# Recurrent merges ahead of the spatial gate, later context transposes and expert shares, and four pieces of elementwise work on GpSimd

## What is computed

```python
y_a = fox_attention(...);  y_b = rg_lru(xb, ...);  y_c = nsa_attention(...);  y_d = spatial_gating(ud, vd, ...)
ys = stack([y_a * silu(ga), y_b * silu(gb), y_c * silu(gc), y_d * silu(gd)], axis=2)
proj = einsum('bsnw,nwd->bsnd', ys, w_branch)                    # n: the four branches
merged = sum(sigmoid(mg.reshape(B, S, 4, D)) * proj, axis=2)     # mg = norm(x) @ w_in[:, mg]
x = x + merged @ w_out
```

```python
x = x + grid_sincos(L)
hc = modulate(rmsnorm(ctx, ...), ...);  keys and values of the context -> state s_f, s_b     # gated linear attention
x = x + mod * mixer_output(...)
gp = probs[idx] / sum(probs[idx])                                # idx: the two chosen experts, gp: their shares
x = x + mod * sum_e gp_e * expert_e(h)
```

## Time and profile before

| | |
|---|---|
| median of 3 runs | 1083.97 us (1081.85 to 1086.04) |
| the profiled execution | 1090.9 us, of which the core's span is 1088.8 us |
| mean granted TensorE clock | 0.955 |
| busy: PE, PEld, DVE, ACT, POOL | 1007.3, 764.9, 612.8, 441.5, 49.5 us |
| chain that ended last | PE 75%, DVE 14%, DMA 6%, ACT 3%, issue 2% |
| HBM read | 221 MB |

### The profile page before, as it was taken

How to read it: one execution, slowest core, us unless ns; L and a number is a source line. 1 busy time by engine, 2 the same in 40 slices (tenths; PEclk the granted TensorE clock), 3 DMA queues, 4 the chain that set the end, 5 groups by cost and what they waited for, 6 DMA issues and landing times.

```text
span 1088.8 us, 13871 instructions
## 1 busy us (share of the span) xinstructions
PE 1007.3 (93%) x5638; PEld 764.9 (70%) x5638; DVE 612.8 (56%) x1065; ACT 441.5 (41%) x709; POOL 49.5 (5%) x66
## 2 busy tenths in 40 slices
PE   7999989999997998898979999995989999999984
PEld 5688667775896988678967886895965753566521
DVE  4777736563655455326574898666842511597605
ACT  4356532954664443124464101335632300556401
POOL 2000000000000000000010222000000000000010
PEclk8999989999998999899989999997899999999987
DMA  9634676765424744624322134002978997999993
GB/s 302 201 135 148 218 267 232 255 224 206 167 78 155 260 166 155 232 86 156 109 95 92 53 141 155 1 1 68 398 292 303 350 382 284 399 404 404 407 350 142
DMA packets 110413, 230.66 MB, mean 212 GB/s; under 512 B 8300, under 2 KB 15757, under 8 KB 110350
## 3 DMA queue, kind: packets, MB, share of 16 engines
q1 hardware_dynamic: 104144, 216.44, 54.8%
q0 software_dynamic: 2880, 9.71, 2.3%
q10 hardware_dynamic: 3326, 3.63, 1.1%
HBM read 221.11 MB, written 8.65 MB: 211 GB/s over the span
## 4 chain that ended last, share of the span: by engine, by line
PE 75%; DVE 14%; DMA 6%; ACT 3%; issue 2%; ACTq 0%; DVEq 0%
PE bank L791 9%; PE bank L1532 7%; PE bank L1533 7%; PE bank L1534 7%; PE bank L2595 6%; PE bank L756 5%; PE bank L2534 4%; PE bank L2535 4%; PE bank L2536 4%; PE bank L2619 3%; DMA more_slots<-in_moe_w_up 2%; PE bank L1446 2%; PE bank L2527 2%; PE bank L1575 2%; PE bank L967 1%
## 5 line engine op out<-in xcount | busy, mean ns | idle before, releaser
L1532 PE MATMUL bank<-rounded 128*128 128x256 f32 (+1 forms) x656 | 201.8, 308 | 9.0 <-DVE slot_rounded L680 4.3
L1533 PE MATMUL bank<-rounded 128*128 128x256 f32 x592 | 168.4, 284 | 0.0
L1532 PEld LDWEIGHTS bank<-rounded 128*128 128x128 f32 x656 | 126.3, 192 | 21.2 <-issue 9.7
L1534 PE MATMUL bank<-rounded,slot_rounded 128*128 128x256 f32 x472 | 134.8, 286 | 0.0
L791 PE MATMUL bank<-x_and_h,slot 128*128 128x256 f32 x544 | 129.1, 394 | 4.9 <-ACT x_and_h L595 4.9
L791 PEld LDWEIGHTS bank<-x_and_h,slot 128*128 128x128 f32 x544 | 106.1, 198 | 22.4 <-issue 7.7
L1533 PEld LDWEIGHTS bank<-rounded 128*128 128x128 f32 x592 | 113.9, 192 | 1.2 <-issue 1.0
L1522 DVE TENSOR_TENSOR slot_rounded<-slot,rounded 128x1024 fp32r<-128x1024 f32 (+1 forms) x63 | 67.1, 1086 | 68.9 <-ACT rounded L1516 68.7
L1534 PEld LDWEIGHTS bank<-rounded,slot_rounded 128*128 128x128 f32 x472 | 91.3, 193 | 0.0
L839 ACT ACTIVATE arena<-bank 128x256 f32<-128x256 f32 x56 | 21.4, 384 | 118.0 <-PE bank L791 96.3
L1516 ACT ACTIVATE rounded<-slot 128x1024 fp32r<-128x1024 f32 (+1 forms) x63 | 57.7, 943 | 27.0 <-PE bank L1534 23.3
(11 more groups left out here) (493 smaller groups left out, 2067.4 us busy)
## 6 DMA issues: line engine op xcount, KB each, us to landing
slot<-in_w_in SPq DMA_DIRECT2D x26, 2048.0 KB, 8.0
slot<-in_ada_w SPq DMA_DIRECT2D x12, 2048.0 KB, 8.4
slot<-in_moe_w_down SPq DMA_DIRECT2D x11, 2048.0 KB, 16.1
more_slots<-in_moe_w_gate SPq DMA_DIRECT2D x8, 2048.0 KB, 15.4
more_slots<-in_moe_w_up SPq DMA_DIRECT2D x8, 2048.0 KB, 18.2
slot<-in_moe_w_gate SPq DMA_DIRECT2D x7, 2048.0 KB, 9.9
x_and_h<-in_moe_w_up SPq DMA_DIRECT2D x6, 2048.0 KB, 15.2
more_slots<-in_moe_w_down SPq DMA_DIRECT2D x5, 2048.0 KB, 17.6
```

The source lines that it names most:

```text
L1532: t.do.matmul(dst, w_hi, x_hi, start=start, stop=False)
L1533: t.do.matmul(dst, w_hi, x_lo, start=False, stop=False)
L1534: return t.do.matmul(dst, w_lo, x_hi, start=False, stop=stop)
```

## The change

Five edits:
1. In `fill` the eight merges of branch 1 move ahead of the gd projections and the four `spatial` products. `merge_start` 1 now stands right behind `spatial_norm` and `h1_split`; `merge_start` 3 stands behind the last `spatial`. As the list over which `ada` is spread is eight jobs shorter, the `ada` jobs lie closer together, and the whole weave from about 107 us on shifts.
2. Of the context, each pair of `ctx_turn` stands one or two projections later.
3. The addition of positions goes from VectorE to GpSimd.
4. For branches 3, 0 and 2, GpSimd makes the low part of the gate's weights (21 instructions of 128x1024); the branch's own low part stays with VectorE. The waits change with it.
5. The shares are computed behind the first two one-hot matrices; scratch buffers are chosen so that the one-hot vectors survive.

```diff
-        spatial = [*ud[2:], *tokens("vd"), ("spatial_norm",), *channels("gd"), *[("spatial", j) for j in range(WT)]]
+        spatial = [*ud[2:], *tokens("vd"), ("spatial_norm",)]
+        gated = [*channels("gd"), *[("spatial", j) for j in range(WT)]]
...
-        fill, scored = spread(early + lru + spatial, ada, 10) + merge[1], attention(UNITS)
+        fill, scored = spread(early + lru + spatial, ada, 10) + merge[1] + gated, attention(UNITS)
...
-        PLAN += woven([*channels("cf0"), ("ctx_scan", 0), ("ctx_turn", 0, 0), ("ctx_turn", 0, 1),
-                       *channels("cf1"), ("ctx_scan", 1), ("ctx_turn", 1, 0), ("ctx_turn", 1, 1), *tokens("cv"),
+        PLAN += woven([*channels("cf0"), ("ctx_scan", 0), ("channels", "cf1", 0), ("ctx_turn", 0, 0), ("channels", "cf1", 1),
+                       ("ctx_turn", 0, 1), *channels("cf1")[2:], ("ctx_scan", 1), ("tokens", "cv", 0), ("ctx_turn", 1, 0), ("tokens", "cv", 1), ("ctx_turn", 1, 1),
                        ("ctx_state", 0), ("ctx_state", 1)], merge[0])
...
-            before = {3: ("merge", 1, KT - 1), 0: ("merge", 3, KT - 1), 2: ("merge", 0, KT - 1)}.get(n, ("merge", n, 0))
+            before = {3: PLAN[PLAN.index(("spatial", WT - 1)) + 1], 0: ("merge", 3, KT - 1), 2: ("merge", 0, KT - 1)}.get(n, ("merge", n, 0))
...
-        @part(VECTOR, "placed")
-        def vector_placed(v):
-            v.wait_ge(*at("position_in"))
-            v.wait_ge(*now("h1"))
-            v.do.tensor_tensor(xT[:, :, :], xT[:, :, :], merged, ALU.add).then_inc(*inc("x_placed"))
+        @part(GPSIMD, "placed")
+        def gpsimd_placed(g):
+            g.wait_ge(*at("position_in"))
+            g.wait_ge(*at("h1", KT - 1))
+            g.do.tensor_tensor(xT[:, :, :], xT[:, :, :], merged, ALU.add).then_inc(*inc("x_placed"))
...
+        def low_name(job, name):
+
+            return "split_gate_low" if job[0] == "merge" and job[1] != BRANCHES[0] and topic_of(name) == "mg" else "split_weights_low"
+
+        def gpsimd_split(g, job):
+            q = SPLITS.index(job)
+            for high, piece, low, name in pieces(job):
+                if low_name(job, name) == "split_gate_low":
+                    g.wait_ge(*at("split_weights_high", q, topic_of(name)))
+                    g.do.tensor_tensor(low, piece, high.bitcast(F32), ALU.subtract).then_inc(*inc("split_gate_low", q, topic_of(name)))
+
+        @part(GPSIMD, "merge_start")
+        def gpsimd_merge_start(g, n):
+            gpsimd_split(g, ("merge", n, 0))
+
+        @part(GPSIMD, "merge")
+        def gpsimd_merge(g, n, dt):
+            job = ("merge", n, dt)
+            if next_split(job):
+                gpsimd_split(g, next_split(job))
+
         def vector_split(v, job):
             q = SPLITS.index(job)
             for high, piece, low, name in pieces(job):
+                if low_name(job, name) == "split_gate_low":
+                    continue
...
-                t.wait_ge(*at("split_weights_low", q, "mg"))
+                t.wait_ge(*at(low_name(job, ("mg", n)), q, "mg"))
...
             v.do.tensor_tensor(chosen, oh1, oh2, ALU.add).then_inc(*inc("moe_chosen"))
-
-
-            for which, oh in enumerate((oh1, oh2)):
-                v.do.tensor_tensor(tmp16, oh, prob, ALU.mult).then_inc(*inc("router_steps"))
...
-            v.do.tensor_tensor(share, share, bcast(total, 1, 2), ALU.mult).then_inc(*inc("router", "shares"))
-
...
-                v.do.tensor_tensor(oh, oh, slot_of, ALU.mult).then_inc(*inc("router_steps"))
+                v.do.tensor_tensor((tmp16, pick)[which], oh, slot_of, ALU.mult).then_inc(*inc("router_steps"))
                 v.wait_ge(*now("router_steps"))
-                v.do.tensor_reduce(slot[:, which], oh, AX_X, ALU.add).then_inc(*inc("router_steps"))
+                v.do.tensor_reduce(slot[:, which], (tmp16, pick)[which], AX_X, ALU.add).then_inc(*inc("router_steps"))
...
             onehot(0)
             onehot(1)
+
+
+            for which, oh in enumerate((oh1, oh2)):
+                v.do.tensor_tensor((tmp16, pick)[which], oh, prob, ALU.mult).then_inc(*inc("router_steps"))
...
+            v.do.tensor_tensor(share, share, bcast(total, 1, 2), ALU.mult).then_inc(*inc("router", "shares"))
+
             gathered(0)
```

More of the change, by code:

```diff
@@ L2810, in vector_experts @@
             v.do.tensor_tensor(chosen, oh1, oh2, ALU.add).then_inc(*inc("moe_chosen"))
-            for which, oh in enumerate((oh1, oh2)):
-                v.do.tensor_tensor(tmp16, oh, prob, ALU.mult).then_inc(*inc("router_steps"))
-                v.wait_ge(*now("router_steps"))
-                v.do.tensor_reduce(share[:, which], tmp16, AX_X, ALU.add).then_inc(*inc("router_steps"))
-                v.wait_ge(*now("router_steps"))
-            v.do.tensor_tensor(total, share[:, 0], share[:, 1], ALU.add).then_inc(*inc("router_steps"))
-            v.wait_ge(*now("router_steps"))
-            v.do.reciprocal(total, total).then_inc(*inc("router_steps"))
-            v.wait_ge(*now("router_steps"))
-            v.do.tensor_tensor(share, share, bcast(total, 1, 2), ALU.mult).then_inc(*inc("router", "shares"))
             for tt in range(NT):
@@ L2893, in vector_experts @@
             onehot(1)
+            for which, oh in enumerate((oh1, oh2)):
+                v.do.tensor_tensor((tmp16, pick)[which], oh, prob, ALU.mult).then_inc(*inc("router_steps"))
+                v.wait_ge(*now("router_steps"))
+                v.do.tensor_reduce(share[:, which], (tmp16, pick)[which], AX_X, ALU.add).then_inc(*inc("router_steps"))
+                v.wait_ge(*now("router_steps"))
+            v.do.tensor_tensor(total, share[:, 0], share[:, 1], ALU.add).then_inc(*inc("router_steps"))
+            v.wait_ge(*now("router_steps"))
+            v.do.reciprocal(total, total).then_inc(*inc("router_steps"))
+            v.wait_ge(*now("router_steps"))
+            v.do.tensor_tensor(share, share, bcast(total, 1, 2), ALU.mult).then_inc(*inc("router", "shares"))
             gathered(0)
```

## The result

| | before | after |
|---|---|---|
| median of four runs each | 1083.18 us (1081.85 to 1086.04) | 1095.67 us (1094.18 to 1099.51) |
| profiled execution, its span | 1090.9, 1088.8 us | 1097.1, 1095.3 us |
| granted TensorE clock | 0.955 | 0.954 |

The ratio is 1.0096 (95% interval 1.0063 to 1.0129): the changed kernel is 10.4 us slower (7 to 14), where 3.8 us faster was forecast. A second comparison further down gives 1.0090. So I read from the traces where time goes, stretch by stretch, and take from the medians how much an edit costs.

What follows compares the result with a forecast made beforehand. TensorE, busy for 93% of the span, was taken as the bound. The terms 7.9 - 11.6 - 2.5 + 3.9 + 10.0 - 2.5 - 2.6 + 1.2 gave +3.8 us off 1084.0, forecast 1080; range 1068 to 1092.

Steps and rivals of the forecast that it cites:

- three signs that the prediction set for itself: Wrong if the stop inside merge 1 0 is missing, the position add leaves VectorE alone, or a GpSimd split exceeds 3 us.
- Edit 1, the stops: Load stop ahead of merge 3 0 goes (+7.9 us); new stops of 9.4 in merge 1 0, 1.8 in merge 3 0.
- Edit 1, the early half: Compression, ada jobs shifted: stops of 2.83, 1.37 and 0.84 us go, 2.2 for xb comes; +3.9 us, -1 to +7.
- Edit 1, what is late next: Behind the products, merge 3 0 stops 1.8 us, -2.5 with slow clock; no later merge of branch 3 got a stop.
- Edit 2: Context: both scan stops, 2.35 and 3.81 us, go with slow clock behind; +10.0 us, bounds 7 to 11.
- Edit 3: Position add: GpSimd takes 4.2 us and holds VectorE 4.1, 1.4 + 0.2 come back; net -2.5 us, +1.4 to -4.4.
- Edit 4: Gate low parts: three stops in branch 2's merges, -1.5 us, and the context's norm 1.1 later; sum -2.6 us.
- Rival C: GpSimd bounds the merges, rounded low parts priced at 3.7 us a piece; 1090 us, chance 12%.
- Edit 5: Shares leave the chain from expert choice to one-hot matrices, 1.36 us; counts late next by 0.15; +1.2 us.
- A: VectorE is not held through GpSimd's position add; 1076 us, chance 15%.
- B: The new stop at merge 1 0 is half as long, ScalarE and VectorE being less loaded; 1074 us, chance 20%.
- D: Loads bind the compression: xb and ada 3 to 6 each 2 us late, slow clock behind; 1088 us, chance 10%.

Runs made afterwards that it cites:

- second comparison: The unchanged changed kernel timed once more against the kernel before: +9.8 us (7.1 to 12.4).
- that half alone: Kernel before with only the ada jobs spread as in the changed kernel; gd, products and merges of branch 1 stay: +2.2 us (-0.9 to 5.3) against before.
- eight pieces: Changed kernel with GpSimd's position addition cut into eight of 256 elements instead of one of 2048: +8.0 us (5.2 to 11.0) against the kernel before.
- the kernel with filler passes: Kernel before with edit 1, the gate passes of merge 1 0 issued three times to fill its stop: +11.3 us (4.9 to 17.7) against before.
- the kernel with ud as cover: Kernel before with edits 1, 2 and 5, ud's last two projections moved behind the norm after vd: -8.5 us (-11.8 to -5.2) against before.

## Why the prediction was wrong, point by point

None of the three signs that the prediction set for itself came: the stop inside merge 1 0 is there, VectorE was held, and a split took 2.4 us. It failed by terms beside those that it watched.

**Edit 1, the stops: right.** 9.62 for 9.4, 2.32 for 1.8, and no load stop at merge 3 0. ScalarE's and VectorE's rows of the changed kernel show the chain that was written down (the exponentials at 284.71, the high part of ys 1, the low parts):

```profile
284.71 0.40 ACT L993 ACTIVATE arena<-arena 128x128 f32<-128x128 f32 x1 [4.82 <-DVE arena L985]
...
285.50 1.04 ACT L1582 ACTIVATE rounded<-arena 128x1024 fp32r<-128x1024 f32 x1
```

```profile
286.57 1.23 DVE L1588 TENSOR_TENSOR rounded<-arena,rounded 128x1024 fp32r<-128x1024 f32 x1 [1.89 <-ACT rounded L1582]
287.71 2.42 DVE L1546 TENSOR_TENSOR slot_rounded<-slot,rounded 128x512 fp32r<-128x512 f32 x3
```

**Edit 1, the early half: failed.** "+3.9; from -1 to +7" measured 0 in the trace of that half alone, and up to 1.7 where the clock stayed up. I had the 2.2 us stop for xb (2.35) and the three that went. What I did not count is that the same shift reorders VectorE's queue ahead of the average of the probabilities: an ada copy (187.46, 0.68 us) now stands right in front of the copy that TensorE waits for, and the stop at L1050 grew from 1.64 to 2.94. How much of the 1.3 us is the copy's, no run isolates. Nor did I count that the 0.84 us stop for ada would stand elsewhere with 0.56 to 0.75. And I booked the slow clock behind the 2.83 stop (2.1) as gained and 1.0 for the one that came, where the rows show 1.7 or nothing, trace by trace.

**Edit 1, what is late next: failed.** I stopped at merge 3 0. Merge 3 1's high part stands in ScalarE's queue behind the exponentials of the next unit and behind an eviction (355.86 to 357.34), so even VectorE's low part comes 1.4 to 1.7 us late, GpSimd's 2.55 to 2.93:

```profile
356.86 0.57 ACT L1031 ACTIVATE arena<-bank 128x512 f32<-128x512 f32 x1
357.34 1.56 ACT L1517 ACTIVATE rounded<-slot 128x1024 fp32r<-128x1024 f32 x2
```

```profile
358.46 2.34 POOL L1528 TENSOR_TENSOR slot_rounded<-slot,rounded 128x1024 fp32r<-128x1024 f32 x1 [317.48 <-ACT rounded L1517]
```

With the clock (0.50 to 0.89 behind 288, 0.66 behind 360) the stretch lost 8.3 us alone and 11.9 beside the other edits, for a forecast of 6.2. Together edit 1 was forecast at 2.3 and cost 12 to 13 by the medians. The failed steps are these two: a gain of 3.9 in the early half that measured 0, and no term for what waits behind merge 3 0. Of the 10 us between, the early half is 3.9 and merge 3 1 is 1.4 to 2.9; up to 3 are slow clock, which no run here isolates; the rest lies in what single traces don't resolve.

**Edit 2: right.** 10 forecast. From the context's norm to the second norm the changed kernel without edit 4 needs 152.9 us and before 164.4, 11.5 less; both scan stops are gone, only 0.34 is left behind cv. With edit 5 the medians say 10.2 (6.5 to 13.8) for 11.2 forecast.

**Edit 3: mechanism right, size off.** "net -2.5" cost 4.6 to 5.0 in the traces and 4.3 to 4.9 in the medians; the seventh piece, forecast at 63.5, came at 66.12. The addition took 4.74, not 4.2, and the 1.6 us I took back "from the missing addition" were not there: in the trace of before VectorE stands idle for 1.19 and 0.69 us for ScalarE right behind the addition, so the addition was covered already. The hold alone is 4.3 to 4.4; the few tenths left fit the half-rate passes behind the 3.19 stop (granted clock 0.57 from 44 to 48 us, before 1.00), which no run isolates. The Trainium skill, page "SBUF — State Buffer", section "SBUF: two separate sides", has the shared pair as an exclusive lock for the whole instruction; the trace agrees for 4.74 us, and with eight pieces the engines took turns piece by piece, which fits that rule.

**Edit 4: mechanism right, size off, two places missed.** The three stops of branch 2 sum to 2.75 for 1.5 forecast, since a piece took 2.42 and not 2.1 us (at 2.6 I had put them at 3.0). The context's norm was not later (1.79 for 1.92), against the 1.1 I gave it. Missing were merge 3 1 and the hold of VectorE, whose branch parts went from 0.68 to 2.04. For merge 3 1 the rows show 1.1 us of GpSimd's; the rest of the 5.4 to 6.0 is not placed. The Trainium skill, page "GPSIMD Engine Reference", section 3.1, gives 4497 ns for an addition of 2048 elements, and by an estimate from it a piece of 1024 takes 2.25 us. The trace has 4.74 us and 2.42. Rival C's price (3.7) was wrong: the rounded output form costs nothing extra that the rows show.

**Edit 5: right.** The gather's stop is 4.01 for 4.98, and from the second norm to the gather it is 1.1 us less, for 1.2. From TensorE's last stop ahead of it (L2486, 752.32 before) to the gather it is 10.8 us in all traces without the edit and 9.4 to 9.7 in those with it.

**Rivals.** A (VectorE not held) and B (the stop half as long) are refuted by the 5.12 and the 9.62. D named the right place, the early half, with a sign nearer the truth, but its 8 us were not there. None had a stop behind merge 3 0. The range was too narrow: its ends moved one or two terms at a time (and the lower one, B with A and edit 2 at 11, adds up to 1069, not 1068), and the early half, what comes late behind merge 3 0, and the two GpSimd prices all failed to the same side.

## What to carry to other kernels

A job that is moved ahead takes its cover along: list what ran on the other engines behind it, and give the waiting chain other work of that length (7.4 us of ud took 7.4 off the stop). Behind a removed stop follow the queue for two jobs more: here the next late pieces took back what was gained. Price work that moves from VectorE to GpSimd by GpSimd's own duration in VectorE's queue wherever VectorE works at the time, also where VectorE is not the bound.

## What the hardware showed unexpectedly

- A one-operand copy on VectorE was held as well as a product, 5.12 us for 0.69, and so were four scans, 4.58 for 2.43. A reduction of 128x1024 beside the eight GpSimd pieces was not (1.22 at 43.23, as before).
- Two engines that take turns slow both: seven GpSimd pieces of 256 took 9.09 us, one instruction with eight times 256 took 4.74 beside a held VectorE.
- The same stop in the same stretch of program can be followed by half-rate passes or not: 2.09 us and then 5.38 for 16 passes in edit 1 alone, 2.30 us and then 3.69 in the kernel with filler passes, whose program differs only later. Of the six traces with this order of jobs and edit 3 left out, three have 5.38 us and three 3.69, behind stops of 1.85 to 3.00 us. What decides it these rows don't show.
- A first matmul at full speed says little. Behind the stop of 2.19 us in the kernel with ud as cover it took 0.36 us, and the granted clock was 0.70 in the first 2 us behind the stop and 0.50 in the next 2.
